# Two weight panels of the neighbourhood layer split ahead of time and reloaded as parts, with VectorE's order around them changed

## What is computed

```
x = layer_norm(alpha * x + (o * silu(gate)) @ w_out)     # end of the attention layer
h = rmsnorm(x, norm_mix_g)
proj = h @ w_in                                          # IN_WIDTH = 2048
u, q, k, v = proj[..., :512], then three times 512
a = pool_mixer(u, w_pool, pool_scale)
b = neighbourhood_attention(q, k, v, rpb)
x = x + concat([a, b]) @ w_out
```

## Time and profile before

| what | value |
|---|---|
| median of three runs | 1425.63 us |
| the profiled execution: its time, its span | 1423.51 us, 1421.7 us |
| granted TensorE clock, all slices | full |
| TensorE busy | 1407.8 us (99%) |
| VectorE busy | 797.8 us (56%) |
| ScalarE busy | 647.8 us (46%) |
| GpSimd busy | 444.2 us (31%) |
| moved by DMA | 239.14 MB, mean 168 GB/s |
| chain that ended last | TensorE 89%, VectorE 7% |

### The profile page before, as it was taken

One profiled execution on the slowest core, in us unless ns is written; L12 is line 12 of the kernel. 1 busy time (PEld: TensorE's weight loads), 2 busy tenths in 40 slices (PEclk: granted clock), 3 DMA queues, 4 the chain that ended last, 5 costly groups with the idle time before them and its releaser, 6 DMA issues.

```text
span 1421.7 us, 18286 instructions
## 1 busy us (share of the span) xinstructions
PE 1407.8 (99%) x6940; PEld 1192.1 (84%) x6940; DVE 797.8 (56%) x1366; ACT 647.8 (46%) x1043; POOL 444.2 (31%) x211
## 2 busy tenths in 40 slices
PE   9999999999999999999999999899999999999998
PEld 7888888888889888888888888678889888888887
DVE  6444353549952746444545479936864111168896
ACT  4323232246554534433444356648954322346554
POOL 5334353441034433343343230135214544410000
PEclk9999999999999999999999999999999999999999
DMA  7267545417432867966796557353126523345552
GB/s 290 89 206 197 187 136 138 135 41 264 168 119 93 300 168 205 298 160 174 204 300 168 151 209 274 118 203 126 51 67 185 149 89 110 126 148 182 203 186 111
DMA packets 43065, 239.14 MB, mean 168 GB/s; under 512 B 4481, under 2 KB 9217, under 8 KB 16897
## 3 DMA queue, kind: packets, MB, share of 16 engines
q1 hardware_dynamic: 30240, 158.85, 31.5%
q0 software_dynamic: 4608, 33.56, 11.7%
q10 hardware_dynamic: 8160, 46.01, 9.3%
HBM read 231.05 MB, written 74.45 MB: 215 GB/s over the span
## 4 chain that ended last, share of the span: by engine, by line
PE 89%; DVE 7%; ACT 1%; DMA 1%; POOL 1%; issue 0%; SPq 0%; DVEq 0%; ACTq 0%; POOLq 0%
PE bank L524 24%; PE bank L523 24%; PE bank L522 24%; PE bank L1073 6%; PE bank L1035 4%; PE bank L1135 3%; PE bank L1052 1%; DVE wlo L1906 1%; DMA v_spill<-v_tok 1%; DVE br_lo L1906 1%; DVE wlo_a L1906 1%; PE bank L821 1%; PE bank L1215 0%; PE bank L923 0%; POOL wlo L688 0%
## 5 line engine op out<-in xcount | busy, mean ns | idle before, releaser
L660 POOL TENSOR_TENSOR wlo<-stage,whi 128x1024 fp32r<-128x1024 f32 (+1 forms) x146 | 361.8, 2499 | 686.6 <-ACT whi L1347 686.6
L522 PE MATMUL bank<-xhi,whi 128*128 128x512 f32 (+1 forms) x504 | 195.1, 387 | 0.0
L524 PE MATMUL bank<-xhi,wlo 128*128 128x512 f32 (+1 forms) x504 | 194.5, 386 | 0.0
L523 PE MATMUL bank<-xlo,whi 128*128 128x512 f32 (+1 forms) x504 | 194.4, 386 | 0.0
L1347 ACT ACTIVATE whi<-stage 128x1024 fp32r<-128x1024 f32 (+1 forms) x150 | 152.2, 1066 | 80.2 <-PE bank L524 61.8
L524 PEld LDWEIGHTS bank<-xhi,wlo 128*128 128x128 f32 x504 | 94.7, 188 | 19.2
L523 PEld LDWEIGHTS bank<-xlo,whi 128*128 128x128 f32 x504 | 94.7, 188 | 19.0
L522 PEld LDWEIGHTS bank<-xhi,whi 128*128 128x128 f32 x504 | 94.7, 188 | 18.7
L2516 DVE TENSOR_TENSOR hid<-relu 128x512 f32 (+1 forms) x32 | 23.2, 724 | 138.1 <-ACT relu L1841 138.1
L522 PE MATMUL bank<-whi,xhi 128*128 128x512 f32 (+1 forms) x236 | 90.4, 383 | 2.4 <-POOL wlo L660 2.4
L524 PE MATMUL bank<-whi,xlo 128*128 128x512 f32 (+1 forms) x236 | 89.7, 380 | 0.0
(11 more groups left out here) (404 smaller groups left out, 3542.6 us busy)
## 6 DMA issues: line engine op xcount, KB each, us to landing
stage<-in_w SPq DMA_DIRECT2D x95, 1024.0 KB, 4.9
tsum<-in_w ACTq DMA_DIRECT2D x32, 1024.0 KB, 14.5
stage<-tsum SPq DMA_DIRECT2D x32, 1024.0 KB, 4.8
tsum<-in_w POOLq DMA_DIRECT2D x16, 1024.0 KB, 10.1
tsum<-tsum POOLq DMA_DIRECT2D x16, 1024.0 KB, 10.0
stage<-in_w SPq DMA_DIRECT2D x8, 1152.0 KB, 5.9
o_spill<-gt SPq DMA_DIRECT2D x16, 256.0 KB, 10.6
bT<-o_spill SPq DMA_DIRECT2D x4, 1024.0 KB, 6.7
```

What stands on the lines that cost most here:

```text
L522: pe.matmul(dst, a_hi, b_hi, start=start, stop=False)
L523: pe.matmul(dst, a_hi, b_lo, start=False, stop=False)
L524: return pe.matmul(dst, a_lo, b_hi, start=False, stop=stop)
L660: pool.tensor_tensor(lo[:, r], stage[p % 2][:, r], hi[:, r].bitcast(F32), ALU.subtract).then_inc(w_lo, 1)
```

## The change

Panels L0 and L0 + 1 are split during the pairs. SyncE loads each into `raw` (new name for the place of `wlo_a`), the first behind panel M0 + 2 and the second in turn (2, 0); ScalarE makes the hi part in `whi_a` at the head of turns (0, 1) and (2, 1); GpSimd makes the lo part in place; SyncE stores both parts to `prep` in DRAM in turns (1, 1) and (3, 1) (2 MB each time). During the seven products GpSimd loads panel L0's parts into new tiles `pre_hi`, `pre_lo` once step 4 is done, and panel L0 + 1's parts into `whi` and `wlo` once step 12 is done. The tiles `pre_hi`, `pre_lo` lie where `bias` will be, so the load of `bias` moves behind the copies of v. `norms` splits no panel. SyncE's loads of L0 + 2 and L0 + 3 move ahead to the end of the seven products.

VectorE's three last sums: `gathers(BO, 1, 13)` (one sum) moves behind `shift(0)`, the two sums on tile `bx` become step 14 and move behind the second `shift`; `gather(q)` waits only for the sums on its own tile. In the first layer the same three sums swap places. TensorE turns tile 1 after two of the four k of `half(1, 0)`. Counters of weights (`at`) and of steps (`op`) become separate bases, since the prepared panels count among the weights.

```diff
+PREP = 14
+Seven = namedtuple("Seven", "dq at op w sums ready banks")
...
         def parts(p):
+            if p == L0:
+                return pre_hi, pre_lo
             if p in APART:
...
+            def prepare(j):
+                sp.dma_start(raw[:, :], t["w"][L0 + j, :, 0:PAN]).then_inc(d_ld[(PREP + j) % 3], 16)
+            def keep_prepared(j):
+                sp.wait_ge(d_tlo, 2 * (PREP + j + 1))
+                sp.dma_start(t["prep"][j, 0, :, :], whi_a[:, :].bitcast(F32)).then_inc(o_st, 16)
+                sp.dma_start(t["prep"][j, 1, :, :], wlo_a[:, :].bitcast(F32)).then_inc(o_st, 16)
             for j in range(6):
                 load(M0 + j, PANEL if j % 3 == 0 else PAN)
+                if j == 2:
+                    sp.wait_ge(b_c, TT)
+                    prepare(0)
-            with sp.Fori(1, PAIRS // 2) as i:
+            for i in range(1, PAIRS // 2):
                 for s in range(2):
                     load(M0 + 3 * s, PANEL, 6 * i)
                     store(2 * i + (s - 2))
+                    if (i, s) == (1, 1):
+                        keep_prepared(0)
+                    elif (i, s) == (2, 0):
+                        sp.wait_ge(o_st, 32)
+                        prepare(1)
+                    elif (i, s) == (3, 1):
+                        keep_prepared(1)
                     load(M0 + 3 * s + 1, PAN, 6 * i)
...
-            for p in range(L0, L0 + 6):
-                if p < L0 + 2:
-                    sp.wait_ge(d_tlo, 2 * (BO.at + 13 + p - L0))
+            for i in range(2):
+                sp.sem_inc(landed[i], 16)
+            for p in range(L0 + 2, L0 + 6):
+                if p < L0 + 4:
+                    sp.wait_ge(d_tlo, 2 * (BO.at + 13 + p - (L0 + 2)))
                 load(p)
...
+            def prepared_lo(j):
+                for b in range(2):
+                    r = slice(b * PAN // 2, (b + 1) * PAN // 2)
+                    pool.wait_ge(d_thi, 2 * (PREP + j) + b + 1)
+                    pool.tensor_tensor(wlo_a[:, r], raw[:, r], whi_a[:, r].bitcast(F32), ALU.subtract
+                                       ).then_inc(d_tlo, 1)
             for m in range(3 * PAIRS):
                 split_lo(M0 + m, PANEL if m % 3 == 0 else PAN)
+                if m in (4, 16):
+                    prepared_lo(m // 12)
...
-            pool.wait_ge(w_lo, 2 * (L0 + 1))
-            for p in range(L0 + 1, L0 + 6):
+            pool.wait_ge(o_st, 64)
+            pool.wait_ge(m_og, 2 * PAIRS + 2)
+            pool.wait_ge(d_pe, BO.op + 5)
+            load_prepared(0)
+            pool.wait_ge(t_sum, 16 * 30)
+            pool.wait_ge(d_pe, BO.op + 13)
+            load_prepared(1)
+            pool.sem_inc(w_lo, 4)
+            for p in range(L0 + 2, L0 + 6):
                 split_lo(p)
...
+                    if turned == 1 and q == 0 and k0 == 0:
+                        pe.wait_ge(t_sum, 16 * (30, 32)[c])
...
-                if turned < 2:
+                if turned == 2:
+                    half(1, 0).then_inc(signal, 1)
+                else:
+                    half(1, 0, 0, 2)
                     turn(1)
-                half(1, 0).then_inc(signal, 1)
+                    half(1, 0, 2, 4).then_inc(signal, 1)
...
                     deviation(0)
-                    split_hi(next_panel, free, done - 1)
                     root_mean_square(0)
...
-                    split_hi(next_panel + 1, free1, done)
...
+                    if (it, s) in ((0, 1), (2, 1)):
+                        prepared_hi(it // 2)
...
+            act.wait_ge(o_st, 64)
             for d in range(2, 14):
...
-            act.dma_start(bias[:, :, :, :], t["bias"]).then_inc(aux["bias"], 16)
-            split_hi(L0 + 2, d_pe, BO.at + 14)
+            act.sem_inc(w_hi, 4)
+            split_hi(L0 + 2, d_pe, BO.op + 14)
             act.wait_ge(aux["wp"], 16)
             for q in range(TT):
                 act.wait_ge(l_v, q + 1)
                 copy(v_tok[:, q, :], E[q][:, :], l_vt)
+            act.dma_start(bias[:, :, :, :], t["bias"]).then_inc(aux["bias"], 16)
...
-                      (4, 4, 8, 9, 10, 11, 11, 12, 12, 13, 13))
+                      (4, 4, 8, 9, 10, 11, 11, 12, 12, 14, 13))
...
+                    dve.wait_ge(d_ev, GATHERS * ln + (15, 16, 18, 18)[q])
                     if q == 0:
-                        dve.wait_ge(d_ev, GATHERS * (ln + 1))
...
                     shift(0)
+                    gathers(BO, 1, 13)
                     gather(1)
                     scale(0)
                     centre(1)
-                    panel_lo()
+                    transposed(0)
                     shift(1)
-                    transposed(0)
+                    gathers(BO, 1, 14)
                     scale(1)
```

More of the change, by code:

```diff
@@ L70 @@
 SUM_OF = (None, 0, 1, 2, None, 3, None)
-Seven = namedtuple("Seven", "dq at w sums ready banks")
-AO = Seven(2, 0, END, 0, (8, 8, 8, 8), ((0, 1), (2, 3), (4, 5), (6, 7), (0, 1), (2, 3), (6, 7)))
-BO = Seven(2, 14, END + 8, 8, (28, 28, 28, 28), ((2, 3), (4, 5), (6, 7), (0, 1), (2, 3), (4, 5), (6, 7)))
-DN = Seven(4, 28, END + 16, 16, (28, 28, 28, 32), ((4, 5), (6, 7), (0, 1), (2, 3), (4, 5), (6, 7), (0, 1)))
+PREP = 14
+Seven = namedtuple("Seven", "dq at op w sums ready banks")
+AO = Seven(2, 0, 0, END, 0, (8, 8, 8, 8), ((0, 1), (2, 3), (4, 5), (6, 7), (0, 1), (2, 3), (6, 7)))
+BO = Seven(2, 16, 14, END + 8, 8, (28, 28, 28, 28), ((2, 3), (4, 5), (6, 7), (0, 1), (2, 3), (4, 5), (6, 7)))
+DN = Seven(4, 30, 28, END + 16, 16, (32, 32, 32, 36), ((4, 5), (6, 7), (0, 1), (2, 3), (4, 5), (6, 7), (0, 1)))
 PANELS = DN.w + 16
@@ L141, in program @@
             wlo_a = sb("wlo_a", [P, PAN], F32R, h)
+        with ExitStack() as h:
+            gap("gap_raw", 128, h)
+            raw = sb("raw", [P, PAN], F32, h)
         with ExitStack() as h:
@@ L227, in program @@
             bx = sb("bx", [P, 2, 2, 512], F32, h)
+            pre_hi = sb("pre_hi", [P, PAN], F32R, h)
+            gap("gap_pre", 320, h)
+            pre_lo = sb("pre_lo", [P, PAN], F32R, h)
         with ExitStack() as h:
@@ L722, in _, with load_prepared @@
             weights_lo(BO, 1)
-            pool.wait_ge(w_lo, 2 * (L0 + 1))
-            for p in range(L0 + 1, L0 + 6):
+            def load_prepared(j):
+                hi, lo = parts(L0 + j)
+                pool.dma_start(hi[:, 0:PAN], t["prep"][j, 0, :, :].bitcast(F32R)).then_inc(t_sum, 16)
+                pool.dma_start(lo[:, 0:PAN], t["prep"][j, 1, :, :].bitcast(F32R)).then_inc(t_sum, 16)
+            pool.wait_ge(o_st, 64)
[7 more added lines that the diff above has]
+            for p in range(L0 + 2, L0 + 6):
                 split_lo(p)
@@ L865, in seven @@
                 f, g = divmod(d, st.dq)
-                pe.wait_ge(d_slo, st.at + d + 1)
+                pe.wait_ge(d_slo, st.op + d + 1)
                 for kk in range(PK):
@@ L1355, in operand_hi @@
                 if d >= 3:
-                    act.wait_ge(d_pe, st.at + d - 2)
+                    act.wait_ge(d_pe, st.op + d - 2)
                 if SUM_OF[f] is not None:
@@ L1531, in _ @@
             norms(0, ln=0, scratch=gate[:, :, :].rearrange("p (t a) n -> p t (a n)", a=2), round_=1, next_panel=B0,
-                  free=d_pe, free1=d_pe, done=AO.at + 13)
+                  free=d_pe, free1=d_pe, done=AO.op + 13)
             act.wait_ge(n_x, TT)
@@ L1572, in _, with prepared_hi @@
                 copy(ql_hi[:, j, :], bank[j][:, :], b_qhi, cols[:, COL_QG + j:COL_QG + j + 1])
+            def prepared_hi(j):
+                act.wait_ge(d_ld[(PREP + j) % 3], 16 * ((PREP + j) // 3 + 2))
+                for b in range(2):
+                    r = slice(b * PAN // 2, (b + 1) * PAN // 2)
+                    copy(whi_a[:, r], raw[:, r], d_thi)
             def pairs(it, last=False):
@@ L1663, in _ @@
             norms(TT, ln=1, rms=0, squares_to=h_tok, scratch=mixT[:, 0:4, :].rearrange("p (t a) n -> p t (a n)", a=2),
-                  round_=2, next_panel=L0, free=d_pe, free1=d_pe, done=BO.at + 13)
+                  round_=2)
             act.wait_ge(r_h, TT)
@@ L1963, in done @@
                 def done(f):
-                    dve.wait_ge(d_pe, st.at + dq * (f + 1))
+                    dve.wait_ge(d_pe, st.op + dq * (f + 1))
                 def product(f, a):
@@ L2226, in _ @@
             combine(AO, 2)
-            dve.wait_ge(d_slo, AO.at + 2)
+            dve.wait_ge(d_slo, AO.op + 2)
             dve.wait_ge(d_tlo, 2 * (AO.at + 2))
@@ L2234, in _ @@
             gathers(AO, 0, 13)
+            gathers(AO, 0, 14)
             dve.wait_ge(aux["rows"], 16)
@@ L2376, in _ @@
             remainders(BO, 13)
-            gathers(BO, 1, 13)
             dve.wait_ge(aux["rows2"], 16)
             dve.wait_ge(aux["grow"], 16)
-            norms(ln=1, rms=0, gb=rows2, centred=h_tok, result=h_tok, round_=2, panel=L0)
+            norms(ln=1, rms=0, gb=rows2, centred=h_tok, result=h_tok, round_=2)
             dve.wait_ge(l_w, 1)
@@ L2541, in _ @@
```

(3 more changed lines are left out.)

16 lines of the change are left out of this document (8 added, 8 removed).

## The result

Over 22 runs of each the changed kernel takes a median of 1425.89 us (1424.14 to 1428.67), the kernel before 1423.76 (1422.69 to 1427.22): ratio 1.0015, 95% interval 1.0009 to 1.0021. That is 2.1 us slower, inside the 0.3% that the forecast called no change. The change was forecast as +1.7. The forecast of the absolute time, 1427.3, is 1.4 too high: the three runs it started from had a median of 1425.63, 1.9 above the longer series, and the change is 0.4 larger than forecast. The profiled execution took 1425.29 us, where 1425.2 was forecast for it.

A forecast was written before the change was run, and what follows sets the result against it. TensorE was taken to bound the kernel, busy 1407.8 of 1421.7 us. A 2.2 us gain against a 3.9 us later store of v made +1.7, so a median of 1427.3 us, range 1420.5 to 1432.5.

The forecast's parts named there:

- The walk of the norms: Norms to first product, timed instruction by instruction: product ends at 941.0 instead of 944.8, undisturbed gain 3.8 us.
- the signs listed: Trace marks of a right forecast: `h_tok` about 911 to 913, product ending 941 to 944, v's store 14 to 15 us.
- Reload of L0: GpSimd's load after step 4 slows step 9's load in a DMA-full stretch: norms 2.6 us late, walk's end 942.6.
- Reload of L0 + 1: GpSimd's load after step 12, beside two panel loads: lands at 918 (914.5 to 920), costs nothing in the walk.
- the gain left: At the start of the neighbourhood layer: TensorE arrives 2.2 us earlier after the reloads' delays.
- `bias`: Its 1.57 MB load right before v's store in ScalarE's queue: store lands 3.9 us later, bounds 0 to 5.5.
- The pairs: Splitting and storing panels there costs 0; the load issued at 575.31 lands near 605 or 606, needed by 610.8.
- The later turn of tile 1: TensorE's turn inside `half(1, 0)`: in the walk or where TensorE has no wait, cost 0.
- A: Rival at v's store: `bias` costs it nothing, its 10.9 us are its own; up to -4.5 us, 1421.1; chance 0.25.
- B: Rival in the pairs: SyncE's queue stays slow, TensorE waits 7 us for the load issued at 575.31; 1434; chance 0.08.
- C: Rival at norms and v's store: norms 4.9 us late, gain 0, `bias` costs 5.5; 1431; chance 0.15.
- D: Rival at GpSimd's DMA issues: busy VectorE holds them up, L0 + 1's parts land at 922; 1429.5; chance 0.07.

The follow-up runs named there:

- experiment 1: Changed kernel with the load of `bias` moved behind the store of v on ScalarE's queue: 1420.77 us, ratio 0.998 against the kernel before.
- experiment 2: Kernel before with only the load of `bias` moved behind the copies of v, in front of the store: 1427.77 us, ratio 1.0028.
- experiment 4: Changed kernel, `bias` load behind the store of v, SyncE's loads of L0 + 2 and L0 + 3 held until L0 + 1's parts landed: 1418.39 us.
- experiment 10: Changed kernel, `bias` load behind the store of v, tile 1 turned before `half(1, 0)` as in the kernel before: 1418.40 us, ratio 0.9965.
- experiment 9: Changed kernel with only SyncE's loads of L0 + 2 and L0 + 3 held until L0 + 1's parts landed, `bias` still before the store: 1424.42 us.
- experiment 7: Changed kernel with the store of L0's parts in turn (1, 1) made twice: 1429.15 us, ratio 1.0041 against the kernel before.
- experiment 8: As experiment 4, but tile 1 turned before `half(1, 0)` as in the kernel before: 1418.27 us, ratio 0.9964 against the kernel before.
- experiment 5: As experiment 4, but VectorE's three last sums in their old order, ahead of `gather(0)`: 1420.99 us, ratio 0.9983 against the kernel before.
- experiment 3: Kernel before with only VectorE's new order of the last three sums: 1421.57 us, ratio 0.9984 against the kernel before.
- experiment 6: As experiment 4, but GpSimd reloads L0's parts after step 8 instead of step 4: 1417.93 us, ratio 0.9957 against the kernel before.

## Why the prediction was right, and where its sizes were off

**The sign and the mechanism** were right: TensorE comes to the neighbourhood layer earlier and the store of v lands later by more. Experiments 1 and 2 show the second by taking the load of `bias` away from the front of the store, and by putting it there alone.

**The walk of the norms** held. It gave 941.0 to 942.6 for the end of the first product and 3.8 us of undisturbed gain; experiment 4, with the disturbances taken away, starts its last copy of v at 941.54 against 945.57, a gain of 4.0. Of the signs listed, those of a right forecast came: `h_tok` of tile 0 at 910.9, the end of the first product near 943.7, the store at 14.4 us, and 4.0 us of waiting at 962 and 970.

**Reload of L0** was put at a delay of 2.6 us. VectorE's first work behind the last lo part started at 902.79 before; now `gather(0)` stands there and starts at 903.85, 1.06 late (at 871 the two executions were level to 0.1). The load of step 9 took 10.2 us, not 8.9, where the sum had taken 11.8. GpSimd's timeline shows why it was less:

```profile
864.77 0.63 POOL L767 DMA_DIRECT2D pre_hi<-prep  x1 [20.40 <-PE bank L533]
873.47 0.54 POOL L768 DMA_DIRECT2D pre_lo<-prep  x1 [8.07 <-issue]
908.30 0.53 POOL L767 DMA_DIRECT2D whi<-prep  x1 [34.29 <-PE bank L533]
908.82 0.54 POOL L768 DMA_DIRECT2D wlo<-prep  x1
```

The second issue stood for 8.07 us, until the first had landed (864.77 + 8.4 = 873.2), so the 2.1 MB did not all come in the load's way. The queues' packets of 870 to 880 (packets, MB, share of 16 engines):

```profile
q1 hardware_dynamic: 233, 1.78, 43.1%
q10 hardware_dynamic: 282, 1.56, 37.9%
q0 software_dynamic: 115, 0.81, 20.6%
```

GpSimd's queue (q0) had 20.6%, not a third. In windows of 1 us it moved packets until 871 and again from 877 on. By the rule of the Trainium skill that the prediction weighed ("DMA: Bandwidth & Descriptors", section "Queues, rings and completion order"), the load would have taken 13.4 us, an estimate. The rule speaks of queues that all have work, and q0 had none for most of 871 to 877, so the case neither bears it out nor speaks against it.

**Reload of L0 + 1** is the step that was off in kind. The prediction had it land at 918, within 914.5 to 920, and said "It costs nothing in the walk, since later waits absorb it". It landed at 919.3, in the range. But the walk had no clock in it: the idle 1.86 us were followed by 3 us at half clock, another 1.7 us of work. Experiments 4 and 10, which remove the wait and the clock's fall in two different ways, both gain 2.4 us over experiment 1. In experiment 9, the changed kernel with this alone taken away, the last copy of v starts 1.8 earlier, at 942.15. Since the delay of the norms was overestimated by 1.5, the gain left came out at 1.66 against 2.2 forecast. Two errors of opposite sign cancelled here, and that the sum came within 0.4 us of the measured change is in part luck.

**`bias`** was put at 3.9, within 0 to 5.5. The store took 3.5 longer. In time the edit is worth +4.4 on the kernel before (experiment 2) and 5.1 on the changed one (experiment 1). In the first a fall of the clock comes on top, which the sum did not have. In the second the store falls by 6.1 us, from 14.4 to 8.3, and not only back to the 10.9 of before, where the load of `bias` was still under way when the store was issued; but TensorE can gain no more than its waits at 962 and 970, 4.0 us, and the two profiled executions differ by 3.4. The rest of the 5.1 shows only in the medians. That the clock falls at these waits in more of the changed kernel's executions than in its profiled one would explain it, and is not shown.

**The pairs** cost nothing, as said. The load of 575.3 took 29.2 us and landed at 604.5 (forecast 605 or 606), 6.3 us before its deadline. Experiment 7 shows that this cover is real and thin: a second store of the same size costs 3.3 us.

**The later turn of tile 1** was put at 0. With `bias` behind the store and the parts late it costs 2.4 (experiment 10 against 1), because it left the gap of the late parts without work. With the parts in time it costs 0 (experiment 8).

**The rivals.** A (the store's 10.9 us are its own) falls by experiments 1 and 2: it is 8.3 with nothing in front and 14.0 to 14.8 with 1.5 MB in front. B (the pairs) did not come, but begins one store further on. C (both collisions at their upper bounds) did not come: 1.06 and 3.5 against 4.9 and 5.5. D (a GpSimd DMA issue well over 0.8 us): one such stall was there, at 873.47, but it ends with the landing of the DMA before it, and did no harm. At 908 the two issues stand 0.52 us apart with VectorE busy, so VectorE's work is not seen to hold them. No row here shows the lockout that the Trainium skill describes in "SBUF — State Buffer", section "SBUF: two separate sides".

**Where the gain went.** Prepared panels with the old order, `bias` behind the store and the hold (experiment 5) give 2.5 us, the order alone (experiment 3) 1.8. The kernel before with `bias` behind the store was not run, so how much of the 2.5 is the preparation's is open; what that edit can remove there is at most the wait of 0.72. With both, `bias` behind the store and no late parts, it is 5.0 to 5.5 (experiments 4, 6, 8, 10). The change as made gives these up to the order of two DMAs in ScalarE's queue and to the early loads of L0 + 2 and L0 + 3.

## What to carry to other kernels

When a load has to move in a queue, look at what stands right behind it: 1.5 MB put ahead of a store that the next layer waits for cost 4 to 5 us, and one line's move behind the store gave it back. Don't start loads that are not yet wanted beside one that is; a wait for the urgent one, or work moved into the gap that it leaves, gave 2.4 us here. When walking a chain, ask of each wait that is left whether TensorE's clock may fall behind it, and look in windows of 1 us, since the average over the page's slices hides it.

## What the runs showed of the hardware

- **The clock behind short waits.** It fell to 0.50 for about 3 us, 1.7 us of work each time, behind idle stretches of TensorE of 1.86 (changed kernel, 919), 2.31 (experiment 1, 919), 2.33 (experiment 5, 912), 2.17 (experiment 9, 960), 2.50 (experiment 7, 964) and 1.85 us (experiment 2, 971). It stayed at 1.00 behind 1.98 (before, 912), 2.12 and 1.84 us (changed kernel, 962 and 970), 2.12 us (experiment 7, 922) and 1.74 us (experiment 2, 963). The length of the stretch alone doesn't decide it, and what does was not settled. Whether it comes in every execution isn't shown either: the changed kernel's 22 runs have mean clocks from 0.996 to 0.999.
- **GpSimd's second DMA issue.** In the reload of L0 the second of two loads was issued only when the first had landed: 8.07 us of standing for a first load of 8.4 us, 7.6 to 8.1 in every other trace with this reload behind step 4, and 4.80 for one of 5.2 in experiment 6, begun 22 us later. In the reload of L0 + 1 the two issues were 0.52 us apart. What differs was not tried.
- **One store, three durations.** The store of v, 1 MB, took 8.1 to 8.3 us with `bias` behind it in the queue, 10.9 with `bias` loading from 939, 14.0 to 14.8 with `bias` issued 0.6 us ahead of it.
